# The causal mask of a kernel's last mixer: from an add on VectorE to 16-bit matmuls into the score bank

## What is computed

```python
s_own = einsum('bhqd,bhkd->bhqk', q, k) * 64 ** -0.5
s_own = where(k_pos <= q_pos, s_own, -inf)
p = softmax(s_own, axis=-1)
primary = einsum('bhqk,bhkd->bhqd', p, v)
mem_out = memory_attention_2(q_mem, ...)          # 4 heads, 256 x 256, no mask
h = h + concatenate([primary, mem_out], -1) @ w_o
h = h + 0.5 * swiglu(rms_norm_2(h, g), ...)
```

## Time and profile before

| | before |
|---|---|
| median of 3 runs | 1833.65 us (1831.34 to 1838.87) |
| the profiled execution's own time | 1838.21 us |
| its span in the trace | 1836.2 us |
| mean granted TensorE clock | 0.979 of full |
| TensorE busy | 1683.2 us (92%) |
| VectorE busy | 962.0 us (52%) |
| ScalarE busy | 693.6 us (38%) |

### The profile page before, as it was taken

How to read it: one execution, slowest core, us unless ns; L and a number is a source line. 1 busy time by engine, 2 the same in 40 slices (tenths; PEclk the granted TensorE clock), 3 DMA queues, 4 the chain that set the end, 5 groups by cost and what they waited for, 6 DMA issues and landing times.

```text
span 1836.2 us, 30802 instructions
## 1 busy us (share of the span) xinstructions
PE 1683.2 (92%) x12728; PEld 1340.8 (73%) x12745; DVE 962.0 (52%) x1561; ACT 693.6 (38%) x1024; POOL 49.3 (3%) x53
## 2 busy tenths in 40 slices
PE   6998989887887878899999899999899998999998
PEld 6987866554545655788888678887788876568887
DVE  4786451111111111666678666666866667746665
ACT  5444441011100101444452264445444454445443
POOL 2000000000000000200002200000000000000000
PEclk9999999999999999999999999999999999899999
DMA  9644369999999999555543045654445643025560
GB/s 303 202 142 149 115 235 423 429 428 429 429 428 429 428 428 394 188 188 170 190 161 115 1 133 188 206 185 136 146 158 200 204 162 115 24 69 172 194 206 23
DMA packets 167979, 409.50 MB, mean 223 GB/s; under 512 B 5351, under 2 KB 137598, under 8 KB 155628
## 3 DMA queue, kind: packets, MB, share of 16 engines
q1 hardware_dynamic: 166048, 404.54, 59.0%
q0 software_dynamic: 1632, 4.01, 0.8%
q10 hardware_dynamic: 236, 0.06, 0.0%
HBM read 407.54 MB, written 1.05 MB: 223 GB/s over the span
## 4 chain that ended last, share of the span: by engine, by line
PE 68%; DMA 19%; DVE 8%; ACT 3%; issue 1%; SPq 0%; ACTq 0%; DVEq 0%
PE bank L1066 18%; DMA odd_expert<-in_w_up_dram 15%; PE bank L1068 9%; PE bank L552 9%; PE bank L554 9%; PE bank L553 9%; DMA odd_expert<-in_w_gate_dram 4%; PE bank L880 3%; PE bank L1050 2%; DVE wlo L1665 2%; PE bank L668 2%; PE bank L694 1%; DVE prob L1928 1%; PE bank L905 1%; ACT whi L1240 1%; PE bank L564 1%
## 5 line engine op out<-in xcount | busy, mean ns | idle before, releaser
L1066 PE MATMUL bank<-x,whi 128*128 128x512 f32 x1408 | 501.3, 400 | 5.3 <-DVE wlo L1665 4.1
L1068 PE MATMUL bank<-x,wlo 128*128 128x256 f32 x1408 | 395.8, 281 | 0.0
L1066 PEld LDWEIGHTS bank<-x,whi 128*128 128x128 f32 x1408 | 265.2, 188 | 73.6 <-DVE wlo L1665 4.4
L2174 DVE TENSOR_TENSOR wlo<-raw,whi 128x2048 fp32r<-128x2048 f32 x120 | 273.9, 2311 | 34.3 <-ACT whi L1542 28.7
L1068 PEld LDWEIGHTS bank<-x,wlo 128*128 128x128 f32 x1408 | 266.6, 189 | 1.5
L1542 ACT ACTIVATE whi<-raw 128x2048 fp32r<-128x2048 f32 x120 | 225.3, 1912 | 60.3 <-PE bank L554 60.3
L1665 DVE TENSOR_TENSOR wlo<-raw,whi 128x2048 fp32r<-128x2048 f32 x67 | 152.7, 2288 | 67.2 <-ACT whi L1240 66.6
L1240 ACT ACTIVATE whi<-raw 128x2048 fp32r<-128x2048 f32 x67 | 127.1, 1909 | 50.9 <-PE bank L554 43.8
L552 PE MATMUL bank<-whi,hh_hi 128*128 128x512 f32 x352 | 138.4, 393 | 0.0
L554 PE MATMUL bank<-wlo,hh_hi 128*128 128x512 f32 x352 | 137.7, 391 | 0.0
L553 PE MATMUL bank<-whi,hh_lo 128*128 128x512 f32 x352 | 137.2, 390 | 0.0
(11 more groups left out here) (305 smaller groups left out, 2354.8 us busy)
## 6 DMA issues: line engine op xcount, KB each, us to landing
raw<-in_ffn_w_gate_dram SPq DMA_DIRECT2D x44, 1024.0 KB, 5.3
raw<-in_ffn_w_up_dram SPq DMA_DIRECT2D x44, 1024.0 KB, 6.4
raw<-in_ffn_w_down_dram SPq DMA_DIRECT2D x44, 1024.0 KB, 5.9
raw<-in_w_gate_dram SPq DMA_DIRECT2D x16, 2048.0 KB, 21.4
raw<-in_w_up_dram SPq DMA_DIRECT2D x16, 2048.0 KB, 24.7
raw<-in_w_down_dram SPq DMA_DIRECT2D x16, 2048.0 KB, 24.9
odd_expert<-in_w_gate_dram SPq DMA_DIRECT2D x16, 2048.0 KB, 26.3
odd_expert<-in_w_up_dram SPq DMA_DIRECT2D x16, 2048.0 KB, 26.4
```

Of the source, the lines that this page charges most:

```text
L1066: pe.matmul(bank[:, :], hi[:, k, :], x_both[x][:, k, :, :].rearrange("p b n -> p (b n)"), start=k == 0, stop=False, skip_group_check=True)
L1068: mm = pe.matmul(bank[:, 0:TOK], lo[:, k, :], xhi[x][:, k, :], start=False, stop=k == KT - 1, skip_group_check=True)
L2174: dve.tensor_tensor(wlo[:, c0_ % SPLIT, :], raw[:, c0_ % RAW, :], whi[:, c0_ % SPLIT, :].bitcast(F32), ALU.subtract).then_inc(lo_ready, 1)
```

## The change

A 16-bit copy of the identity and of the 128x128 causal mask is made once, at the start, on VectorE. For the 12 causal heads of the last mixer, TensorE adds the mask to each diagonal block of the scores by a matmul of identity and mask that accumulates in the bank; the product of the last 128 queries with all 256 keys becomes two of 128 columns each, since only the second takes the mask. VectorE takes both maxima from the bank and scales them (`masked_max`), and writes no scaled copy of the scores; ScalarE reads the bank with scale 0.125 in causal heads too, and its wait for a free buffer (`t_done`) moves with that from VectorE to ScalarE.

```diff
+        ident_b, mask_b = sb("ident_b", [P, P], BF16), sb("mask_b", [P, P], BF16)
...
-            def causal_scores(q, k):
-                scores([(slice(0, 128), [(q[:, 0:P], k[:, 0:P])]), (slice(128, 384), [(q[:, P:TOK], k[:, 0:TOK])])])
+            def causal_scores(q, k, masked=False):
+                parts = [(slice(0, 128), [(q[:, 0:P], k[:, 0:P])]), (slice(128, 384), [(q[:, P:TOK], k[:, 0:TOK])])]
+                if masked:
+                    parts = [(slice(0, 128), [(q[:, 0:P], k[:, 0:P]), (ident_b[:, :], mask_b[:, :])]),
+                             (slice(128, 256), [(q[:, P:TOK], k[:, 0:P])]),
+                             (slice(256, 384), [(q[:, P:TOK], k[:, P:TOK]), (ident_b[:, :], mask_b[:, :])])]
+                scores(parts)
...
-                return lambda: causal_scores(qb_t[half, head // 2, :], kb_t[half, head // 2, :]), CAUSAL_BLOCKS, out
+                return lambda: causal_scores(qb_t[half, head // 2, :], kb_t[half, head // 2, :], True), CAUSAL_BLOCKS, out
...
-                        if widths[s] == CAUSAL_W:
-                            exps(CAUSAL_W, prob_slot(n["unit"]), 1.0, False)
-                        else:
-                            full_exps(0.125)
+                        exps(widths[s], ps[4 + n["unit"] % 2], 0.125, True)
...
+            def masked_max(scale):
+
+                u = n["unit"]
+                dve.wait_ge(s_full, u + 1)
+                nm, bank = nmax[:, stat_cols(u)], ps[4 + u % 2]
+                dve.tensor_reduce(nm[:, 0:1], bank[:, 0:P], AX, ALU.max, negate=True)
+                link(dve.tensor_reduce(nm[:, 1:2], bank[:, P:CAUSAL_W], AX, ALU.max, negate=True))
+                dve.tensor_scalar(nm, nm, scale, None, ALU.mult).then_inc(nm_ready, 1)
+                n["unit"] += 1
...
+            dve.wait_ge(in_c, 16)
+            dve.tensor_copy(ident_b[:, :], ident)
+            dve.tensor_copy(mask_b[:, :], cst[:, C_CAUSAL:C_CAUSAL + P])
             normed_rows(h)
...
-                        if widths[s] == CAUSAL_W:
-                            causal_max(cst[:, C_CAUSAL:C_CAUSAL + CAUSAL_W], 0.125, 1.0)
-                        else:
-                            full_max(0.125)
+                        (masked_max if widths[s] == CAUSAL_W else full_max)(0.125)
```

## The result

| | before | after |
|---|---|---|
| median | 1833.94 us (13 runs, 1831.24 to 1838.87) | 1839.92 us (13 runs, 1834.49 to 1842.24) |
| the profiled execution's own time | 1838.21 us | 1836.1 us |
| its span | 1836.2 us | 1834.1 us |
| mean granted clock of it | 0.979 | 0.979 |

The ratio is 1.0024, with an interval of 1.0013 to 1.0034: the changed kernel is slower by some 4.4 us (2.4 to 6.2 us), by less than 0.5%. The two profiled executions stand the other way round, 2 us apart, so the traces cannot be compared by their ends. They have to be compared stage by stage, at the same granted clock.

A forecast was written before the change was run, and what follows sets the result against it. TensorE was taken to bound nine of the twelve causal heads. Its added work, +3.5 us, less 0.4 and 0.2 us of VectorE relief, gave +2.9 us on 1833.65, so 1836.5 us, range 1829 to 1843 us.

The forecast's parts named there:

- The bound: Last mixer: TensorE ends last in nine of twelve causal heads, heads 3 to 11; VectorE is not waited for there.
- The cost of a step: TensorE, steady causal heads: 0.33 us more per head at full clock, between 0.21 and 0.41.
- signs of being wrong: Mask matmul above 0.15 us, steady steps not longer by 0.2 to 0.4 us, or the chain there leaving TensorE.
- the split: TensorE, causal scores: a 256-column product turned into two of 128 costs 0.11 us more per head.
- the two mask matmuls: TensorE, causal scores: two identity-times-mask matmuls at 0.11 us each, 0.22 us per head.
- The page weighed there: Skill page on weight-load overlap, speaking for the mask matmul's upper bound of 0.15 us; the transposes were held against it.
- VectorE: Causal heads: VectorE held for 0.73 us instead of 1.11, 0.38 us less per head.
- The sum: Whole kernel: +3.5 us on TensorE, -0.4 in head 1, -0.2 for waits on ScalarE's copy, +2.9 us.
- the two heads at half clock: Two of the nine steady causal heads run at half clock, where the addition is 0.61 us each.
- The dips: Half-clock stretches around the steady part's start, behind idle gaps of 2.36 and 2.39 us; forecast kept about the length seen.
- the first rival: Clock dip shrinks or goes as TensorE's gaps shorten: 1829 to 1831 us with both dips gone; chance 0.27.
- The premise that a gap of 1.51 us is followed by no dip: TensorE's idle gaps before the steady part: dips followed 2.36 and 2.39 us, none followed 1.51 us.

The follow-up runs named there:

- experiment 2: Kernel before, with maxima and exponentials of causal heads reading the bank, TensorE's products unchanged and the mask left out: 1832.79 us, 0.9991 of before.
- experiment 3: Changed kernel with each mask matmul issued twice in a row, four per head: 1841.57 us, 1.0038 of the kernel before.
- experiment 5: Changed kernel with both mask matmuls over only the 64 rows of the scores' operands, half the queries unmasked: 1839.23 us, one run.
- the pair with filled gaps: Kernels before and after, each with filler matmuls in TensorE's three idle gaps ahead of the steady part: 1831.39 and 1834.91 us.
- experiment 1: Kernel before, with only the 256-column score product of causal heads split into two of 128, VectorE still adding the mask: 1832.26 us, 0.9997.

## Why the prediction was right, and where not

The forecast was 1836.5 us, the range 1829 to 1843, and within 0.5% with a chance of 0.93. Measured: 1839.92 us and +0.24%. The class was safe, since nothing that moves a few microseconds of 1834 reaches 0.5%; what counts is whether the terms held. In turn:

- **The bound.** Right. TensorE ends last in the steady steps, before and after; work added there shows, work taken from VectorE does not (experiment 2).
- **The cost of a step.** The size was off: 0.33 us forecast, 0.41 as upper bound, 0.42 measured. Two of the signs of being wrong that the prediction names came true: a mask matmul costs more than 0.15 us (0.41 / 2 = 0.2), and the steps are longer by more than 0.4 us. Both terms of it were wrong, in opposite directions, and that they partly cancel is luck: the split costs 0.01 instead of 0.11, the two mask matmuls 0.41 instead of 0.22. I had priced a mask matmul by the transpose and the filler, at 0.11 us. Both stand in these rows behind other matmuls of 128 rows; the mask matmul stands between products of 64. The nearest row by size was not the nearest by what stands before and behind it.
- **The page weighed there.** The Trainium skill, TensorE: Matmul & The Clock Gate, Part 3, lets a weight load overlap matmuls in flight only when the row groups differ. For that I had 0.15 us a mask matmul, with its load exposed, as the upper bound, and set it aside. Its number was nearer, and where the identity follows a product of 64 rows the trace agrees: the load starts only with its matmul (1580.10 us). But experiment 3 has a second identity load on the same 128 rows hide in full (0.055 us a matmul), and in experiment 5 the load over the same 64 rows starts 0.11 us ahead; by the page's rule both would be exposed. There the measurement decides against the rule: here loads were hidden where the rows stayed the same, and not where they changed. The transposes that the prediction held against it stand behind matmuls of the same 128 rows.
- **VectorE.** 0.73 us a head, as forecast.
- **The sum.** +2.9 us forecast; without the two heads at half clock that would be 9 x 0.33 - 0.6 = +2.4. The steps as measured give 9 x 0.42 - 0.6 = +3.2 at full clock, the pair with filled gaps 3.5, the plain pair 4.4 (2.4 to 6.2). The 1.2 us between the last and the step count may be heads at half clock, each worth twice; the interval is too wide to say so. The medians stand further apart, 6.0 us, than the ratio does (4.4 us); the forecast is 3.4 us under the measured median, and its change 1.5 us under that of the ratio.
- **The dips.** The profiled execution fitted the first rival: one dip gone, the other 6.64 us instead of 10. The runs do not: over 13 runs the granted clock was 0.977 to 0.980, over 35 runs of the kernel before 0.976 to 0.982, and no gain shows in the time. The premise that a gap of 1.51 us is followed by no dip also fell. In experiment 1 both gaps of 2.34 and 1.50 us are followed by one, while the same gap of 1.50 us in experiment 2 is not:

```profile
1552.00:1555.00 3.00, 3.00 (x9) 0.96 (x8) 2.84 (x8) 2.18 (x6) 0.00 (x0) 0.63 0.01 3
1555.00:1558.00 3.00, 3.00 (x11) 1.45 (x10) 0.69 (x1) 0.76 (x2) 0.00 (x0) 0.80 0.00 0
...
1562.86:1566.50 3.64, 3.64 (x7) 1.28 (x8) 3.57 (x8) 0.29 (x1) 0.00 (x0) 0.53 0.07 15
```

So the length of the gap alone does not decide. That fits what the Trainium skill, TensorE: Matmul & The Clock Gate, Part 1, says of a watch that runs freely against the program. What is shown is that with the three gaps ahead of the steady part at 0.75 us or less there was no dip, in five traces.

## What to carry to other kernels

Before work is moved from a half-idle engine to the one on the chain, ask what the receiving engine pays for it in that place, not what such an instruction costs elsewhere: the same mask cost 0.42 us a head as two matmuls, one among products of another row count, and 0.11 us as one matmul next to its own kind. A relief for an engine that nobody waits for is worth nothing until the bound is cut as well: only with filler taken from TensorE did it shorten the steps (2.40 against 2.50 us), and in the time even that is hardly seen. And where runs of one kernel spread more than the change in question, look for what spreads them (here the granted clock behind idle gaps): with that gone, 3.5 us could be read from 12 runs each.

## What the runs showed of the hardware

- A matmul of 128 columns over 128 rows between products over 64 rows cost about 0.1 us more on each side than the same over the same 64 rows (0.42 and 0.16 us against 0.32 and 0.06). Its weight load started only with its matmul behind a product of 64 rows (1580.10 us), and 0.11 us ahead of it where both used the same 64 rows (1587.35 and 1587.46 us). The change from 32-bit to 16-bit operands alone shows little: 0.18 us for two matmuls, of which 0.11 are their columns. This rests on one trace of each.
- A weight load of 128 rows behind another matmul on the same rows hid in full: 0.055 us for a further matmul of 128 columns.
- Without the 16-bit filler, and with the gaps ahead of the loop unfilled, the granted clock stayed at the 1.2 GHz level for some 50 us with TensorE busy throughout, in both traces; by their times 15 of 20 runs were of that kind; with one or two such matmuls a step, and the gaps filled, it stayed at 2.4 GHz.
